# A hybrid attention, GLA, mLSTM and MoE block: first unit by feature tiles, mLSTM normaliser as a column of ones

## The reference

```python
def rmsnorm(x, g):
    xf = x.astype(jnp.float32)
    y = xf * lax.rsqrt(jnp.mean(xf * xf, axis=-1, keepdims=True) + EPS)
    return (y * g.astype(jnp.float32)).astype(x.dtype)
...
    z = _split_in(h @ w_in + b_in)
...
    num = (w_inter[..., None] * jnp.einsum('bhcid,bhcde->bhcie', qc, c_prev)
           + jnp.einsum('bhcij,bhcje->bhcie', w_intra, vc))
    den = w_inter * jnp.einsum('bhcid,bhcd->bhci', qc, n_prev) + jnp.sum(w_intra, axis=-1)
    h = num / jnp.maximum(jnp.abs(den), jnp.exp(-m_i))[..., None]
```

## Time and profile before

| | us |
|---|---|
| Median of 3 runs | 1564.58 (1563.92 to 1565.61) |
| Profiled execution, its own time | 1564.46 |
| Its span in the trace | 1562.80 |
| TensorE busy | 1521.1 |
| VectorE busy | 1231.1 |
| ScalarE busy | 945.8 |

### The profile page before, as it was taken

How to read it: one execution, slowest core, us unless ns; L and a number is a source line. 1 busy time by engine, 2 the same in 40 slices (tenths; PEclk the granted TensorE clock), 3 DMA queues, 4 the chain that set the end, 5 groups by cost and what they waited for, 6 DMA issues and landing times.

```text
span 1562.8 us, 19329 instructions
## 1 busy us (share of the span) xinstructions
PE 1521.1 (97%) x7552; PEld 1272.0 (81%) x7552; DVE 1231.1 (79%) x1214; ACT 945.8 (61%) x872; POOL 34.6 (2%) x66
## 2 busy tenths in 40 slices
PE   6999999999999999999899999999999999999995
PEld 5898888888887898888688888888888888888884
DVE  5679876654547688866798998989989899899995
ACT  5346534544444356634677777777777777777774
POOL 2000000000000000000100000000000000000000
PEclk9999999999999999999899999999999999999997
DMA  7444445454555444544999998999989999899960
GB/s 272 178 154 172 179 168 189 171 190 184 192 185 185 175 182 153 194 161 152 373 366 375 357 367 327 360 377 353 368 325 351 386 352 369 319 363 378 353 251 29
DMA packets 113938, 411.66 MB, mean 263 GB/s; under 512 B 13168, under 2 KB 13216, under 8 KB 113840
## 3 DMA queue, kind: packets, MB, share of 16 engines
q1 hardware_dynamic: 111152, 401.73, 69.1%
q0 software_dynamic: 2688, 8.61, 1.7%
HBM read 409.24 MB, written 1.05 MB: 263 GB/s over the span
## 4 chain that ended last, share of the span: by engine, by line
PE 92%; DVE 4%; ACT 2%; issue 1%; DMA 1%; SPq 0%; DVEq 0%; ACTq 0%
PE ps L988 31%; PE ps L621 20%; PE ps L999 14%; PE ps L889 8%; PE ps L611 4%; PE ps L903 4%; PE ps L600 3%; DVE w_lo L1510 1%; PE ps L949 1%; PE ps L1016 1%; PE ps L958 1%; DVE w_lo L1373 1%; ACT w_hi L1063 1%; DMA raw_m<-dense_dram 1%; PE ps L579 1%
## 5 line engine op out<-in xcount | busy, mean ns | idle before, releaser
L1510 DVE TENSOR_TENSOR w_lo<-late,w_hi 128x2048 fp32r<-128x2048 f32 x192 | 438.0, 2289 | 39.7 <-ACT w_hi L1123 39.7
L1123 ACT CAST w_hi<-late 128x2048 fp32r<-128x2048 f32 x192 | 367.3, 1913 | 41.7 <-PE ps L988 41.7
L1373 DVE TENSOR_TENSOR w_lo<-raw_m,w_hi 128x2048 fp32r<-128x2048 f32 x117 | 267.3, 2290 | 141.4 <-ACT w_hi L1063 141.0
L1063 ACT CAST w_hi<-raw_m 128x2048 fp32r<-128x2048 f32 x117 | 222.0, 1906 | 142.7 <-PE ps L621 67.8
L988 PE MATMUL ps<-w_hi,hT_hi 128*128 128x512 f32 x704 | 281.8, 400 | 2.9 <-DVE w_lo L1510 2.9
L988 PE MATMUL ps<-w_hi,hT_lo 128*128 128x512 f32 x704 | 274.8, 390 | 0.0
L988 PE MATMUL ps<-w_lo,hT_hi 128*128 128x512 f32 x704 | 274.7, 390 | 0.0
L621 PE MATMUL ps<-w_hi,hT_hi 128*128 128x512 f32 x480 | 190.7, 397 | 2.1 <-DVE w_lo L1373 1.2
L621 PE MATMUL ps<-w_hi,hT_lo 128*128 128x512 f32 x480 | 187.7, 391 | 0.0
L621 PE MATMUL ps<-w_lo,hT_hi 128*128 128x512 f32 x480 | 187.7, 391 | 0.0
L1510 DVE TENSOR_TENSOR w_lo<-raw_m,w_hi 128x2048 fp32r<-128x2048 f32 x72 | 165.0, 2292 | 24.6 <-ACT w_hi L1123 24.6
(11 more groups left out here) (332 smaller groups left out, 2100.9 us busy)
## 6 DMA issues: line engine op xcount, KB each, us to landing
late<-experts_dram SPq DMA_DIRECT2D x384, 512.0 KB, 4.9
raw_m<-dense_dram SPq DMA_DIRECT2D x234, 512.0 KB, 4.0
raw_m<-experts_dram SPq DMA_DIRECT2D x144, 512.0 KB, 4.8
bias<-b_in_dram POOLq DMA_DIRECT2D x26, 256.0 KB, 4.6
xt<-x_dram SPq DMA_DIRECT2D x4, 256.0 KB, 5.6
out_dram<-xn SPq DMA_DIRECT2D x4, 256.0 KB, 2.5
tmp<-w_small_dram POOLq DMA_DIRECT2D x2, 320.0 KB, 4.0
tmp<-ffn_norm_g_dram POOLq DMA_DIRECT2D x1, 512.0 KB, 3.9
```

The costliest lines, as they stand in the source:

```text
L1063: copy(w_hi[:, g % RS, :], slot_raw(g, False)).then_inc(hi_ready, 1)
L1123: copy(w_hi[:, m % RS, :], slot_raw(m, True)).then_inc(hi_ready, 1)
L1373: tt(w_lo[:, g % RS, :], slot_raw(g, False), w_hi[:, g % RS, :], ALU.subtract)\
L1510: tt(w_lo[:, m % RS, :], slot_raw(m, True), w_hi[:, m % RS, :], ALU.subtract).then_inc(lo_ready, 1)
```

## The change

What it does, in parts:

- **Front.** The host adds an array `front`: the gains of the first norm and x with features on partitions. SP first issues five pieces of it, each followed by the matching pieces of chunks 0 and 1 (feature tiles 0, 1, 2 to 3, 4 to 5, 6 to 7), then chunk 2, the constants, all of x, and chunk 3 once `lo_ready` is 1. TensorE does 20 transposes of the identity and then unit `mq` tile by tile (`first_unit`, six matmuls for each of eight feature tiles); ScalarE and VectorE split x and weights tile by tile. The 16 transposes of x in layer 0 are gone.
- **Chunk 3.** In layer 0 ScalarE and VectorE split chunks 2 and 3 before the squares and the norm.
- **GpSimd.** The bias, small weights, gate weights and rope are issued after the last piece has landed.
- **Row scale.** `rb` stands after both chunks of `mk`, in both layers.
- **Normaliser.** `vl` has 130 columns for each head, the last two of them ones; the 12 products have 130 columns and the 12 products by `ones` are gone. Results lie in four banks in place of three, and VectorE works in four parts.

The diff, cut to its core:

```diff
+    WARM = 20
+    PIECES = ((0, 1), (1, 2), (2, 4), (4, 6), (6, 8))
+    VC = 130
...
-                ("up1", (0, 1, 2, 3)), ("mo", (4, 5, 6)), ("g2", (0, 1)), ("yT2", (4, 5)), ("up2", (6, 7, 0, 1)),
+                ("up1", (0, 1, 2, 3)), ("mo", A4), ("g2", (0, 1)), ("yT2", (4, 5)), ("up2", (6, 7, 0, 1)),
...
-        vl = piece(NT * MIX).rearrange("p (t n) -> p t n", t=NT)
+        vl = piece(NT * 4 * VC).rearrange("p (t h n) -> p t h n", t=NT, h=4)
...
+        front = tmp[:, 1024 - KT:1024 + KT * T]
+        gains = front[:, 0:KT]
+        xT = front[:, KT:KT + KT * T].rearrange("p (k n) -> p k n", k=KT)
...
-            sp.dma_start(cols[:, :, :], cols_d.rearrange("l p n -> p l n")).then_inc(c_in, 16)
-            load_x(0)
-
             def load(g):
 
                 for h in range(2):
                     c = slice(h * CK // 2, (h + 1) * CK // 2)
                     sp.dma_start(slot_raw(g, False)[:, c], dense_d[g, h]).then_inc(raw_in[g % RM], 16)
 
+            for i, (k0, k1) in enumerate(PIECES):
+                c = slice(KT + k0 * T if k0 else 0, KT + k1 * T)
+                sp.dma_start(front[:, c], front_d[:, c]).then_inc(xT_in[i], 16)
+                c, d = slice(k0 % 4 * W, ((k1 - 1) % 4 + 1) * W), slice(k0 % 2 * W, ((k1 - 1) % 2 + 1) * W)
+                sp.dma_start(raw_m[:, k0 // 4, c], dense_d[k0 // 4, k0 % 4 // 2][:, d]).then_inc(piece_in[i], 16)
             for l in range(L):
                 for n in range(2 * NU):
                     g = LAYER_BASE[l] + n
+                    if g < 2:
+                        continue
                     if g >= RM:
                         sp.wait_ge(lo_ready, g - RM + 1)
                     load(g)
-                    if g == 0:
+                    if g == 2:
+                        sp.dma_start(cols[:, :, :], cols_d.rearrange("l p n -> p l n")).then_inc(c_in, 16)
+                        load_x(0)
                         load_x(1)
...
-            pool.dma_start(ws_raw, w_small_d[0]).then_inc(ws_in, 16)
-            pool.dma_start(gw[0:16, :], gate_w[0]).then_inc(ws_in, 16)
-            pool.dma_start(bias[:, 0, :], b_in[0, OFF["mq"]:OFF["mq"] + W].partition_broadcast(P))\
-                .then_inc(bias_in[0], 16)
-            pool.dma_start(rope[:, :, :, :], rope_d).then_inc(c2_in, 16)
             nc.gpsimd.memset(ones[:, :], 1.0)
+            nc.gpsimd.memset(vl[:, :, :, P:VC], 1.0)
...
+            pool.wait_ge(piece_in[-1], 16)
+            pool.dma_start(bias[:, 0, :], b_in[0, OFF["mq"]:OFF["mq"] + W].partition_broadcast(P))\
+                .then_inc(bias_in[0], 16)
+            pool.dma_start(ws_raw, w_small_d[0]).then_inc(ws_in, 16)
+            pool.dma_start(gw[0:16, :], gate_w[0]).then_inc(ws_in, 16)
+            pool.dma_start(rope[:, :, :, :], rope_d).then_inc(c2_in, 16)
...
+            def first_unit():
+
+                for k in range(KT):
+                    pe.wait_ge(h0_lo, k + 1)
+                    if k % 4 == 3:
+                        pe.wait_ge(lo_ready, k // 4 + 1)
+                    else:
+                        pe.wait_ge(piece_lo, k + 1 - k // 4)
                     for t in range(NT):
-                        await_drained(l - 1, "acc", 2 * h + t)
-                else:
-                    pe.wait_ge(x_in[h], 16 * NT)
-                transposes(l, "norm", xt, h)
+                        b = FILL[0, "mq", t][0]
+                        for pa, (a, r) in enumerate(for_3):
+                            ins = mm(ps[:, b, :], hT[a][:, k, t * P:(t + 1) * P],
+                                     wsp[r][:, k // 4, k % 4 * W:(k % 4 + 1) * W],
+                                     start=(k == 0 and pa == 0), stop=(k == KT - 1 and pa == 2))
+                        if k == KT - 1:
+                            done(ins, 0, "mq", t)
+                    if k == 3:
+                        ins.then_inc(w_used, 1)
...
-            for h in range(2):
-                norm_transposes(0, h)
+            for i in range(WARM):
+                nc.tensor.transpose(ps[:, 7, 0:P], ident[:, :], ident[:, :])
+            first_unit()
             for l in range(L):
-                chunk(l, "mq", 0, "norm", between=(lambda: norm_transposes(l, 1)) if l else None)
-                chunk(l, "mq", 1, "norm")
-                chunk(l, "mk", 0)
+                if l:
+                    chunk(l, "mq", 0, "norm", between=lambda: norm_transposes(l, 1))
+                    chunk(l, "mq", 1, "norm")
+                unit(l, "mk")
                 pe.wait_ge(rb_ready, l + 1)
                 b = claim(l, "rb")
                 for t in range(NT):
                     ins = mm(ps[:, b, t * P:(t + 1) * P], rcol[:, t, :], ident[:, :], start=True, stop=True)
                 done(ins, l, "rb")
-                chunk(l, "mk", 1)
                 pe.wait_ge(ws_ready, l + 1)
...
-                att_values(l, "mo", mW, vl)
-                b = claim(l, "mo", 2)
-                for h in range(4):
-                    mm(ps[:, b, h:h + 1], mW[:, h, 0:P], ones[:, 0:1], start=True, stop=True)
-                    mm(ps[:, b, 4 + h:5 + h], mW[:, h, P:2 * P], ones[:, 0:1], start=True, stop=False)
-                    ins = mm(ps[:, b, 4 + h:5 + h], mW[:, h, 2 * P:3 * P], ones[:, 0:1], start=False, stop=True)
-                done(ins, l, "mo", 2)
+                for q in range(4):
+                    b = claim(l, "mo", q)
+                    for hh in range(2):
+                        h = 2 * (q % 2) + hh
+                        o = ps[:, b, hh * VC:(hh + 1) * VC]
+                        if q < 2:
+                            ins = mm(o, mW[:, h, 0:P], vl[:, 0, h, :], start=True, stop=True)
+                        else:
+                            mm(o, mW[:, h, P:2 * P], vl[:, 0, h, :], start=True, stop=False)
+                            ins = mm(o, mW[:, h, 2 * P:3 * P], vl[:, 1, h, :], start=False, stop=True)
+                    done(ins, l, "mo", q)
...
-            act.wait_ge(c_in, 16)
+            for k in range(KT):
+                i = [k0 <= k < k1 for k0, k1 in PIECES].index(True)
+                act.wait_ge(xT_in[i], 16)
+                A(hT_hi[:, k, :], xT[:, k, :], ACT.Copy, scale=gains[:, k:k + 1]).then_inc(h0_hi, 1)
+                act.wait_ge(piece_in[i], 16)
+                c = slice(k % 4 * W, (k % 4 + 1) * W)
+                copy(w_hi[:, k // 4, c], raw_m[:, k // 4, c]).then_inc(hi_ready if k % 4 == 3 else piece_hi, 1)
+            nsplit[0] = 2
             for l in range(L):
 
-                for i in range(2):
-                    hi_of(l, "norm", i, hT_hi, C_AG)
-                split_to(LAYER_BASE[l])
                 if l:
+                    for i in range(2):
+                        hi_of(l, "norm", i, hT_hi, C_AG)
+                    split_to(LAYER_BASE[l])
                     load_sqrt()
-                for i in range(2, 4):
-                    hi_of(l, "norm", i, hT_hi, C_AG)
-                split_to(LAYER_BASE[l] + 1)
+                    for i in range(2, 4):
+                        hi_of(l, "norm", i, hT_hi, C_AG)
+                    split_to(LAYER_BASE[l] + 1)
+                else:
+                    ahead(l, "mq")
+                    act.wait_ge(c_in, 16)
+                    for h in range(2):
+                        act.wait_ge(x_in[h], 16 * NT)
                 squares(0)
                 squares(1)
...
-            dve.wait_ge(c_in, 16)
+            for k in range(KT):
+                dve.wait_ge(h0_hi, k + 1)
+                stt(hT_lo[:, k, :], xT[:, k, :], gains[:, k:k + 1], hT_hi[:, k, :], ALU.mult, ALU.subtract)\
+                    .then_inc(h0_lo, 1)
+                c = slice(k % 4 * W, (k % 4 + 1) * W)
+                if k % 4 == 3:
+                    dve.wait_ge(hi_ready, k // 4 + 1)
+                else:
+                    dve.wait_ge(piece_hi, k + 1 - k // 4)
+                tt(w_lo[:, k // 4, c], raw_m[:, k // 4, c], w_hi[:, k // 4, c], ALU.subtract)\
+                    .then_inc(lo_ready if k % 4 == 3 else piece_lo, 1)
+            nsplit[0] = 2
             for l in range(L):
-                for i in range(2):
-                    lo_of(l, "norm", i, hT_hi, hT_lo, C_AG)
-                split_to(LAYER_BASE[l])
                 if l:
+                    for i in range(2):
+                        lo_of(l, "norm", i, hT_hi, hT_lo, C_AG)
+                    split_to(LAYER_BASE[l])
                     for t in range(NT):
                         b = await_full(0, "acc", 2 + t)
                         tt(xt[:, t, W:D], xt[:, t, W:D], ps[:, b, :], ALU.add).then_inc(drained[b], 1)
-                for i in range(2, 4):
-                    lo_of(l, "norm", i, hT_hi, hT_lo, C_AG)
-                split_to(LAYER_BASE[l] + 1)
-                ahead(l, "mq", 0)
+                    for i in range(2, 4):
+                        lo_of(l, "norm", i, hT_hi, hT_lo, C_AG)
+                    split_to(LAYER_BASE[l] + 1)
+                else:
```

(30 more changed lines are left out.)

31 lines of the change are left out of this document (22 added, 9 removed).

## The result

The changed kernel takes 1553.18 us (median of 4 runs, 1551.95 to 1554.71), against 1565.0 us for the kernel before on the same chip: a ratio of 0.9923, 95% interval 0.9911 to 0.9936. It is faster by about 12 us, 2 us more than the 9.8 us forecast, and inside the range. The same kernel taken again later on (the last experiment) gave 1552.71 us, 0.9921 (0.9907 to 0.9936).

What follows compares the result with a forecast made beforehand. TensorE was taken to bound the kernel (92% of the chain of waits), its start bound by bytes in flight. Front 4.6 plus normaliser 5.2 gave 9.8 us: 1564.46 - 9.8 + 0.12 = 1554.8 us, range 1551.2 to 1558.6 us.

Steps and rivals of the forecast that it cites:

- So TensorE sets the pace once it is at speed: First unit: TensorE's 1.37 us per feature tile outlasts loading and splitting, so `mq` ends at about 17 us.
- Chunk 3: Start: chunk 3 lands at 23.6 us behind the extra x; with 4.3 us of splitting, second `mk` chunk starts at 27.9.
- Nothing else in the way: Before `mv`: ScalarE's squares and bias and VectorE's chunk 4 subtraction finish by 36.6 us with TensorE, costed at nothing.
- The move of `rb`: Row scale placed behind both `mk` chunks: costs zero, at worst 1 us.
- The term of 1.7 us: TensorE's clock falls about the 3.4 us wait before `mk`'s second chunk; slow matmuls cut the front from 6.3 to 4.6 us.
- Likeliest case: Whole kernel: front 4.6 us with the clock's fall, normaliser 5.2 us, 9.8 us together, 1554.8 us; chance 0.47.
- first rival, The clock holds: Wait before `mk` short enough or clock holds; chunk 3 lands at 22.5 us, front brings 7.4 us: 1552.0 us; chance 0.24.
- The normaliser: Attention, each layer: 12 one-column products removed, 2.6 us; wider columns and VectorE's extra work cost nothing; 5.2 us in all.
- Small pieces move slowly: Start: at 302 GB/s chunk 3 lands 3.9 us later, front brings nothing, 1559.4 us; half that delay 1557.2; chance 0.17 both.
- Normaliser kept back: Normaliser: VectorE or wider columns keep back 0.6 to 2.6 us in each layer, 1556 to 1560 us; chance 0.08.
- The clock never rises: First units: 96 matmuls of `mq` and `mk` run 0.43 us apart, total about 1570 us, slower than before; chance 0.04.

Runs made afterwards that it cites:

- the last experiment: Changed kernel timed and profiled once more, unchanged (beside a kernel joining two other edits): 1552.71 us, ratio 0.9921.
- second trace: Profile from the repeat of the changed kernel, one of its shortest executions: 1551.85 us, span 1550.1 us.
- first trace: First profile of the changed kernel, the longest of its four executions: 1554.71 us, span 1552.90 us.
- experiment 1: The two halves in separate kernels: kernel before plus normaliser part only, 1558.58 us; changed kernel without the normaliser part, 1561.49 us.
- experiment 2: Changed kernel plus identity transposes in TensorE's waits, 16 ahead of tile 2 and 30 ahead of the second `mk` chunk: 1553.43 us, ratio 0.9928.
- experiment 4: Changed kernel with four pieces of two feature tiles each in place of five pieces: 1551.67 us, ratio 0.9919.
- experiment 5: Changed kernel without the 20 identity transposes ahead of the first matmul: 1555.0 us, ratio 0.9940.
- experiment 6: Changed kernel with the transposed row scale `rb` put back between the two chunks of `mk`: 1558.95 us, ratio 0.9961.
- the front alone: Changed kernel with the old normaliser (products by ones, three banks): 1561.49 us, ratio 0.9976; its trace is of a 1559.01 us execution.
- the normaliser alone: Kernel before with only the normaliser part added (130 columns, ones in `vl`, four banks): 1558.58 us, ratio 0.9959.
- experiment 7: Changed kernel with constants and token-major x loaded behind chunk 3, and GpSimd's loads issued later too: 1551.09 us, ratio 0.9911.

## Why the prediction came out as it did

**The start.** First matmul at about 6 us: 5.77. `mq` ending at about 17 us: 18.9 in the second trace, 21.6 in the first. The step that failed is "So TensorE sets the pace once it is at speed": the pieces set it up to tile 2. They moved at 278 GB/s in place of the 359 used, and were 1.5 us late by that (9 slices of 0.75 us, 81 GB/s missing, 0.55 MB). That did no harm in the second trace, for what `mq` lost came out of the waits for chunks 2 (0.96 us left, forecast 2) and 3 (2.42 left, forecast 3.4).

**Chunk 3.** Forecast 23.6 us, with 21.2 and 27.5 as bounds: 23.7 and 24.8 us, and 23.3 to 24.2 us in the traces of experiments 1, 2, 4, 5 and 6. That it came so close is in part luck: in the second trace the pieces fell short of 359 GB/s by 0.5 MB (288), the 19 slices behind them were above it by 0.6 MB (399), and 7.9 MB had moved when chunk 3 landed, where the sum counted 7.52. Its split and the three hand-overs took 4.3 us as forecast. Second chunk of `mk`: forecast 27.9, 28.03 and 29.11 us. `mv` with a fast clock: forecast 36.6, measured 37.04.

**Nothing else in the way.** Right: the bias of `mq` and the subtraction of chunk 4 were forecast for 36.6 us, and end at 36.4 us (34.12 + 2.28) in the first trace, ahead of `mv`. The move of `rb` costs nothing; that it is worth some 5 us once x comes late (experiment 6) the prediction didn't say.

**The clock.** The term of 1.7 us stands in one trace and not in the other. (The prediction names slow matmuls behind the longer wait as a sign of being right and a pace of 0.43 us past 20 us as a sign of being wrong; both are the same event.) In the first, 24 matmuls took 7.37 us, 1.9 over the 5.46, behind a wait of 1.88 us; the clock also fell behind tile 2, by 1.6 us, which the wait for chunk 3 partly hid. In the second the clock held behind a longer wait (2.42 us), and in the front alone behind 1.97. The wait's length thus doesn't decide it. Of the rule in the Trainium skill, "TensorE: Matmul & The Clock Gate", section on oscillation, the traces show both sides: waits for DMA between bursts do let the clock fall, in some executions; in others, with the same program, they don't. Likeliest case and first rival are hence both true, each of one of the two profiled executions. The error of about 2 us in the median has two parts, as far as the traces show: this term, which should have stood below its full price, and the 1.4 us below. How the other executions divide isn't shown.

**The normaliser.** 2 x 2.6 = 5.2 us: 2.7 and 2.7 in the traces; alone 5.9 us (4.4 to 8.4 by the interval). VectorE needs 2.45 us from the first row sum to the last `ytok` (225.10 to 226.13 + 1.42), and the transposes came at 234.71 us without a wait, six microseconds after the last `ytok` was multiplied by its gate (227.46 + 1.28) where five were forecast.

**What the sum left out.** The router and the end. Before, the clock there was 0.50 from 758 us to after 766; in the second trace it is back at 1.00 from 754 us, 3.2 us after the gathers start, where it was about 5 us before. The last matmuls of the program, in the first trace of the changed kernel and in that of before:

```profile
1537.05 0.50 PE L1001 MATMUL ps<-ysb_hi,yT_hi 128*128 128x512 f32 x1 [0.31 <-DVE xt L1933]
1537.38 0.40 PE L1001 MATMUL ps<-ysb_lo,yT_hi 128*128 128x512 f32 x1
1537.64 0.50 PE L1001 MATMUL ps<-ysb_hi,yT_hi 128*128 128x512 f32 x1
```

```profile
1546.15 0.80 PE L958 MATMUL ps<-ysb_hi,yT_hi 128*128 128x512 f32 x1
1546.74 0.63 PE L958 MATMUL ps<-ysb_lo,yT_hi 128*128 128x512 f32 x1
1547.17 0.63 PE L958 MATMUL ps<-ysb_hi,yT_hi 128*128 128x512 f32 x1
```

0.33 and 0.26 us apart there, 0.59 and 0.43 here. But the traces of experiments 2, 6 and 7, which have the change, and that of the front alone end at the slow pace, and the normaliser alone at the fast one. So no trace shows this to be an effect of the change; it moves by up to 1.4 us in a comparison of two executions. With it the sums close: 3.2 + 2.7 + 2.7 + 0.6 + 0.7 = 9.9 us of span for the first trace, 5.9 + 2.7 + 2.7 + 0.8 + 0.6 = 12.7 us for the second.

**The rivals.** *The clock holds*, 1552.0 us: its clock half was right in some executions, its chunk 3 at 22.5 us wasn't. *Small pieces move slowly*: the pieces did (278 GB/s, worse than the 302 it took), but the chunks behind them made up for it at 380 to 432, so chunk 3 was at most 1.2 us late. *Normaliser kept back*: didn't happen. *The clock never rises*: it had risen by the third matmul in both traces (0.23 us apart from 6.42 and 6.56 us on), and without the warm-up (experiment 5) after seven.

The Trainium skill, "DMA: Bandwidth & Descriptors", section "Measured (HBM→SBUF, 128 partitions, SWDGE, issued from GpSimd)", asks for batches of 1 MiB or more. On that the trace agrees only in its direction: the pieces of 0.13 to 0.5 MB, which SyncE issues, went at 236 to 320 GB/s, the 0.5 MB halves of whole chunks at 380 to 432. Two tiles per piece from the start is already enough to see (experiment 4).
